# Attention weights turned through three rotating PSUM banks, with the mixed output in a bank of its own

## What is computed

```python
o_cmp, p_cmp = nsa_compressed(q, k_c, v_c, cmp_pos, cmp_w1, cmp_w2, slopes)
o_sel = nsa_selected(q, k_s, v_s, p_cmp, slopes)
o_win = nsa_window(q, k_w, v_w, slopes)
g = jax.nn.sigmoid(gate_logit.reshape(B, T, N_HEADS, 3))
o = g[..., 0:1] * o_cmp + g[..., 1:2] * o_sel + g[..., 2:3] * o_win
return o.reshape(B, T, MIX_WIDTH) * jax.nn.silu(z)
```

## Time and profile before

| what | value |
|---|---|
| median of 3 runs | 2367.28 us (2366.47 to 2367.64) |
| span of the profiled execution, first to last instruction | 2361.6 us |
| median minus that span | 5.7 us |
| busy share of the span: TensorE matmul, VectorE, ScalarE | 95%, 42%, 21% |
| the attention stage in the span, first scores to last gated output | 2173.1 to 2238.9 us |

### The profile page before, as it was taken

The page is one execution under the profiler, slowest core; times in us unless marked ns, Lnnn a source line. Parts: engine busy times, 40 slices in busy tenths (PEclk is TensorE's granted clock), DMA queues, the critical chain, the costliest instruction groups (busy, mean ns, idle before and its releaser), DMA issues.

```text
span 2361.6 us, 31308 instructions
## 1 busy us (share of the span) xinstructions
PE 2247.6 (95%) x13240; PEld 1193.1 (51%) x13240; DVE 998.6 (42%) x1839; ACT 504.0 (21%) x909; POOL 6.0 (0%) x10
## 2 busy tenths in 40 slices
PE   8999999999999989998999999899999999999797
PEld 2443454444443335756444433337884447786545
DVE  6569543211112117975011112136752446545574
ACT  3275000211111102142111111111112321113601
POOL 0000000000000000000000000000000000000000
PEclk9999999999999999999999999999999999999999
DMA  8623435799999995284999999952221220121252
GB/s 315 224 72 123 167 133 242 291 424 427 428 427 427 426 413 214 87 344 171 401 428 427 428 427 428 427 240 72 89 90 53 81 75 27 53 80 73 69 190 72
DMA packets 73528, 565.96 MB, mean 240 GB/s; under 512 B 11081, under 2 KB 12105, under 8 KB 40683
## 3 DMA queue, kind: packets, MB, share of 16 engines
q1 hardware_dynamic: 64928, 540.33, 57.3%
q10 hardware_dynamic: 7596, 20.47, 2.3%
q0 software_dynamic: 864, 3.15, 0.3%
HBM read 547.67 MB, written 14.68 MB: 238 GB/s over the span
## 4 chain that ended last, share of the span: by engine, by line
PE 71%; DVE 12%; DMA 11%; ACT 3%; issue 2%; SPq 0%; ACTq 0%; DVEq 0%
PE bank L219 70%; DMA experts<-in_exp_w 6%; DMA fast_w<-in_w_in 2%; DMA wring<-in_w_small 1%; PE bank L222 1%; DMA cf_wmod<-in_w_mod 1%; DVE cf_y L2124 1%; DVE scores L3579 0%; DVE residual L1842 0%; ACT wring L1770 0%; DVE fast_s L2381 0%; DVE fast_s L2378 0%; DVE fast_s L2380 0%; DVE fast_s L2379 0%; ACT scores L3631 0%
## 5 line engine op out<-in xcount | busy, mean ns | idle before, releaser
L219 PE MATMUL bank<-normed,wring 128*128 128x512 f32 (+2 forms) x960 | 379.6, 579 | 0.7 <-ACT normed L377 0.5
L219 PE MATMUL bank<-experts,wring 128*64 128x512 f32 x1632 | 360.1, 594 | 15.0 <-DMA experts<-in_exp_w 14.7
L1805 DVE TENSOR_TENSOR squares<-squares,bank 128x512 f32<-128x512 f32 x32 | 22.0, 688 | 662.8 <-ACT squares L1799 662.8
L219 PEld LDWEIGHTS bank<-normed,wring 128*128 128x128 f32 (+1 forms) x960 | 158.4, 181 | 182.8 <-issue 172.9
L219 PEld LDWEIGHTS bank<-experts,wring 128*64 128x64 f32 x1632 | 115.1, 137 | 252.1 <-issue 227.8
L219 PE MATMUL bank<-experts,hs_t 128*64 128x512 f32 (+1 forms) x832 | 169.8, 562 | 0.6 <-DMA experts<-in_exp_w 0.2
L219 PE MATMUL bank<-rms,y 128*128 128x512 f32 x256 | 123.0, 604 | 4.5 <-DVE residual L1842 4.5
L1842 DVE SCALAR_TENSOR_TENSOR residual<-bank,mods,residual 128x512 f32<-128x512 f32 x128 | 96.1, 751 | 73.0 <-PE bank L219 65.7
L1799 ACT ACTIVATE squares<-bank 128x512 f32<-128x512 f32 x32 | 19.1, 597 | 483.5 <-PE bank L219 483.5
L219 PEld LDWEIGHTS bank<-experts,hs_t 128*64 128x64 f32 x832 | 58.2, 137 | 105.8 <-issue 98.6
L219 PE MATMUL bank<-proj 64*64 64x64 f32 (+1 forms) x2192 | 92.0, 233 | 5.8 <-ACT proj L3200 4.8
(11 more groups left out here) (638 smaller groups left out, 2835.6 us busy)
## 6 DMA issues: line engine op xcount, KB each, us to landing
experts<-in_exp_w SPq DMA_DIRECT2D x146, 2048.0 KB, 21.1
spare<-in_exp_w SPq DMA_DIRECT2D x20, 2048.0 KB, 21.8
normed<-in_exp_w SPq DMA_DIRECT2D x20, 2048.0 KB, 20.4
wring<-in_w_in SPq DMA_DIRECT2D x44, 512.0 KB, 4.1
wmod<-in_w_mod SPq DMA_DIRECT2D x16, 1024.0 KB, 6.2
residual<-in_w_mod SPq DMA_DIRECT2D x16, 1024.0 KB, 6.6
cf_wmod<-in_w_mod SPq DMA_DIRECT2D x16, 1024.0 KB, 9.8
fast_w<-in_w_in SPq DMA_DIRECT2D x30, 512.0 KB, 4.4
```

The source lines that it names most:

```text
L219: return self.nc.tensor.matmul(out, lhsT, rhs, start=start, stop=stop, skip_group_check=True)
L1805: k.vec(v.tensor_tensor(m.hs[:, e, :], m.hs[:, e, :], k.bank[3 - 2 * e][:, :], ALU.mult), f"{m.name}.hs{i}.{e}")
```

## The change

The blocks of each head are cut into parts of up to four blocks (`parts_of`): one part for each head in units 0 and 1, two in the others. Parts are numbered through all units (`part_number`); part x is transposed into bank 4 + x % 3, and waits for the copy of part x - 3. ScalarE waits for each part by itself and copies it with one instruction; a short block in a part with others is copied with them, on all 128 partitions. Bank 7 holds the mixed output alone, and the wait for the output of the unit before, ahead of the fifth block of head 1, is gone. Instructions after the changed functions stand 13 to 17 lines further down (the exponentials at L3648, the copies at L3658).

```diff
--- before.py
+++ after.py
@@ -3510,30 +3510,47 @@
     ins.then_inc(*k.up("tensor", f"at{n}.scores"))
 
 
+def parts_of(m, n):
+
+    last = len(blocks_of(m, UNITS[n][0])[2]) - 1
+    return [(e, o, min(o + 4, last + 1), o == last) for e in range(2) for o in range(0, last + 1, 4)]
+
+
+def part_number(m, n, i):
+
+    return sum(len(parts_of(m, x)) for x in range(n)) + i
+
+
 def turned_weights_tensor(k, m, n):
 
-    t, bank = k.nc.tensor, k.bank
-    c, hp, u = UNITS[n]
+    t, (c, hp, u) = k.nc.tensor, UNITS[n]
+    blocks = blocks_of(m, c)[2]
     t.wait_ge(*k.at(f"at{n}.weights"))
-    for e in range(2):
-        for j, (o, w, _) in enumerate(blocks_of(m, c)[2]):
-            if n and e == 1 and j == 4:
-                t.wait_ge(*k.at(f"at{n - 1}.out"))
-            ins = k.turn(bank[4 + 2 * e + j // 4][0:w, (j % 4) * P:(j % 4 + 1) * P], m.sc[:, u + e, o:o + w])
-        ins.then_inc(*k.up("tensor", f"at{n}.turned{e}"))
+    for i, (e, lo, hi, _) in enumerate(parts_of(m, n)):
+        x = part_number(m, n, i)
+        if x >= 3:
+            t.wait_ge(*k.at(f"at.part{x - 3}"))
+        for j in range(lo, hi):
+            o, w, _ = blocks[j]
+            ins = k.turn(k.bank[4 + x % 3][0:w, (j - lo) * P:(j - lo + 1) * P], m.sc[:, u + e, o:o + w])
+        ins.then_inc(*k.up("tensor", f"at.turned{x}"))
+
+
+def mixed_bank(k):
+    return k.bank[7][:, 0:P]
 
 
 def mixed_tensor(k, m, n):
 
-    t, bank = k.nc.tensor, k.bank
+    t = k.nc.tensor
     c, hp, u = UNITS[n]
     blocks = blocks_of(m, c)[2]
-    t.wait_ge(*k.at(f"at{n}.pt1"))
+    t.wait_ge(*k.at(f"at.part{part_number(m, n + 1, 0) - 1}"))
     if n:
         t.wait_ge(*k.at(f"at{n - 1}.out"))
     for j, (o, w, val) in enumerate(blocks):
         for e, r in enumerate(HALVES):
-            ins = k.mm(bank[7][r, 0:P], val, m.pt[0:w, e, j * P:(j + 1) * P], j == 0, j == len(blocks) - 1)
+            ins = k.mm(mixed_bank(k)[r, :], val, m.pt[0:w, e, j * P:(j + 1) * P], j == 0, j == len(blocks) - 1)
     ins.then_inc(*k.up("tensor", f"at{n}.mixed"))
 
 
@@ -3603,7 +3620,7 @@
     c, hp, u = UNITS[n]
     cols = slice(c * P, (c + 1) * P)
     v.wait_ge(*k.at(f"at{n}.mixed"))
-    k.vec(v.tensor_tensor(m.ys[:, 6 + hp, cols], k.bank[7][:, 0:P], m.pj[:, NZ + hp, cols], ALU.mult), f"at{n}.out")
+    k.vec(v.tensor_tensor(m.ys[:, 6 + hp, cols], mixed_bank(k), m.pj[:, NZ + hp, cols], ALU.mult), f"at{n}.out")
 
 
 def attention_vector(k, m, filler):
@@ -3634,15 +3651,11 @@
 
 def turned_weights_scalar(k, m, n):
     s = k.nc.scalar
-    c, hp, u = UNITS[n]
-    j = len(blocks_of(m, c)[2]) - 1
-    for e in range(2):
-        bb, pt = (k.bank[4 + 2 * e], k.bank[5 + 2 * e]), m.pt[:, e, :]
-        s.wait_ge(*k.at(f"at{n}.turned{e}"))
-        for o in range(0, j, 4):
-            w = min(4, j - o)
-            k.act(s.copy(pt[:, o * P:(o + w) * P], bb[o // 4][:, 0:w * P]))
-        k.act(s.copy(pt[0:NCMP, j * P:(j + 1) * P], bb[j // 4][0:NCMP, (j % 4) * P:(j % 4 + 1) * P]), f"at{n}.pt{e}")
+    for i, (e, lo, hi, alone) in enumerate(parts_of(m, n)):
+        x = part_number(m, n, i)
+        rows = NCMP if alone else P
+        s.wait_ge(*k.at(f"at.turned{x}"))
+        k.act(s.copy(m.pt[0:rows, e, lo * P:hi * P], k.bank[4 + x % 3][0:rows, 0:(hi - lo) * P]), f"at.part{x}")
 
 
 def attention_scalar(k, m, filler):
```

## The result

| what | before | with the change |
|---|---|---|
| median of five runs each, side by side | 2367.28 us (2365.81 to 2368.47) | 2374.65 us (2371.57 to 2378.08) |
| ratio, with its 95% interval | | 1.0040 (1.0029 to 1.0051) |
| the profiled execution: span | 2361.6 us | 2376.8 us (2378.08 us in all) |
| VectorE's first biases to the last gated output | 64.48 us | 73.14 us |

The account below looks back on a forecast made before the run. A circle of waits between VectorE and ScalarE was taken to set the pace. Terms -0.36 + 1.52 + 1.80 - 0.49 = +2.47 us, with one clock fall at 1.0, made +3.5: 2370.8 us, range 2367.0 to 2375.5.

Parts of the forecast that it names:

- the clock's term: TensorE's longer pauses before the fourth parts, units 2 to 6: one fall of the granted clock, +1.0 us.
- Rival 1: The clock falls in several units: three falls, +5.5 to +9.7 us, taken as 2374; chance 0.32.
- the forecast: Attention stage: the new wait binds and the clock falls at most once, +1.7 to +4.7 us; chance 0.61.
- The waits: Attention stage, sum without the clock: delays in units 2 to 6 less gains in units 0 and 7, +2.47 us.
- Unit 7: From mixed(6) to mixed(7): TensorE's own work sets 5.58 us instead of 6.07, so -0.49 us.
- Copies merged in unit 0: ScalarE's copies ahead of the gate activation: two take 1.02 us where four took 1.38, -0.36 us.
- Around the span: Outside the profiled span: 5.7 us added to get from the forecast span to the median.
- The upper bound: Transposes and scores behind a pause: one clock fall can at most double them, +2.4 us.

Follow-up runs that it names:

- e5_filled_less: The changed kernel with two unread constant matmuls ahead of the fourth part of units 2 to 6: 2368.94 us beside 2366.50, ratio 1.0009.
- e6_change_again: The changed kernel, unaltered, run again on the same chip as the filled ones: 2372.39 us beside 2366.50, ratio 1.0029.
- e4_wait_alone: The kernel before, plus a wait of head 1's fifth block for its own unit's first copy: 2375.41 us beside 2367.21, ratio 1.0032.
- e7_filled_but_one: e5_filled_less without the filling matmuls in unit 6: 2369.82 us beside 2366.50, ratio 1.0016.
- e3_filled: The changed kernel with four unread constant matmuls ahead of the fourth part of units 2 to 6: 2376.37 us beside 2367.21, ratio 1.0036.
- e1_old_banks: The changed kernel's parts and merged copies, but with the banks and wait of the kernel before: 2365.32 us beside 2367.21, ratio 0.9987.

## Why the prediction was wrong

The direction and the mechanism came out, the size didn't. **The step that failed is the clock's term**: "I take one fall, at 1.0, a little under the middle". The profile shows four falls of some 1.6 us each, 6.5 in all. Rival 1, the clock falling in several units, was the outcome; it had 0.32, the forecast 0.61. That its taken value, 2374, lies so near the measured 2374.65 is partly luck: it counted three falls, and the same kernel measured again had 2372.39.

- **The waits, forecast +2.47.** With the clock held (e5_filled_less) the units take, against before, 0.41, 0.14, 0.62 and 0.48 us more in units 2 to 5 (forecast 0.38, 0.11, 0.58, 0.45), 1.80 in unit 6 (forecast 1.80) and 0.33 less in unit 7 (forecast 0.49 less). With the 0.36 of unit 0 the sum is +2.76. Timed it is 2.4 us, or 2.1 by the ratio with -0.2 to 4.3. These terms were right.
- **Unit 7** came out 0.16 dearer: mixed(7) starts 2251.07 - 2245.33 = 5.74 us after mixed(6), and I had reckoned 5.58. TensorE's own work is what it waits for, as forecast, without a gap:

```profile
2247.38 2.04 PE L222 MATMUL bank<-consts,scores 128*128 128x128 f32 x16
2249.26 1.88 PE L219 MATMUL bank<-mixer_out,proj 128*128 128x512 f32 x4
```

  From start to start the transposes took 1.88 us, for 1.80 reckoned, and the four steps of the branch product 1.81, for 1.74.
- **Copies merged in unit 0, forecast -0.36.** The two copies take what I took them for, and the gate activation now starts at 2191.14, 1.02 us after the first copy, where before it was 1.38:

```profile
2190.12 0.99 ACT L3658 COPY scores_t<-bank 128x384 f32<-128x384 f32 x2 [0.40 <-ACT squares L2580]
```

- **The clock, forecast one fall at 1.0.** Four falls, each against the same unit of e5_filled_less: 1.62, 1.50, 1.68 and 1.70 us, 6.5 in all, and 0.14 ahead of unit 2. With the waits, 2.76 + 6.50 + 0.14 makes 9.40; 0.75 goes off, since the profiled execution of before lost that much itself ahead of unit 2 (14.26 us there, against 13.15 without a fall, plus the 0.36 that ScalarE's copies took longer); the 8.65 left stand beside 73.14 - 64.48 = 8.66. For e6_change_again it is 2.76 + 4.08 - 0.75 = 6.09 beside 6.10. This splits the difference over its causes; it is no check of them, for the terms are themselves differences between rows of the table. The check is e5_filled_less: with the clock held the falls' share is gone and the waits are the forecast's.

- **Around the span** I took 5.7 us, the median less the profiled span. In the change it is 1.3 us, so most of the 5.7 was that one execution being quicker than the median. The sum was made against the median too and isn't touched by it.

Two errors made the clock's term small. The count: from one row on either side I held a pause short of the 3.9 us of unit 0 to be half safe, and took one fall for three like pauses. It isn't that the pauses came out longer: they were 2.97 us in unit 2 (3.37 in e6_change_again) for 3.4, and 2.44 (1.46) in unit 4 for 3.1; a pause of 1.78 us in unit 3 still lost the clock. The price: I took 1.0 as the middle between nothing and 2.4, but for scores with no slack left behind them a fall costs nearly its own lost work: eight steps of the branch products took 5.29 instead of 3.60. The upper bound held: the dearest fall, in unit 5 of e6_change_again, cost 2.06.

The length of the pause alone doesn't tell which unit loses the clock. In the change 2.97, 1.78, 2.48 and 2.37 us lost it and 2.44 didn't; in e6_change_again 3.37, 2.80 and 2.48 lost it, 1.46 and 1.58 didn't; in e4_wait_alone 3.43, 2.12, 2.67 and 2.46 lost it, 2.08 didn't; in e7_filled_but_one the one left, 2.37, lost it. The shorter ones are oftener safe, but 1.78 wasn't, and the 3.53 us of unit 0 were safe in e6_change_again. What decides in the single case stays open. So 12 of these 16 pauses lost the clock; of the 14 that were filled, in e3_filled, e5_filled_less and units 2 to 5 of e7_filled_but_one, none did.

The Trainium skill ("TensorE: Matmul & The Clock Gate", A second HAM failure mode: psum-queue depth-cycling) tells of a kernel that cycles through banks and idles between groups often enough for the clock to swing between its two levels. The traces agree here: in units 2 to 6 the clock goes from 1.00 to 0.50 and back four times in one execution and three in another. The rotation by itself isn't what does it: e4_wait_alone rotates no bank and loses as much, 1.0032 against 1.0029 and 1.0040.

The Trainium skill ("Perfetto Trace Analysis", Optimizing Tensor Performance, Matmuls) has independent groups rotate through banks so that the copy of one overlaps the next. Here the copy has to wait for the exponentials ahead of it on ScalarE, so with three banks for four parts TensorE waited for ScalarE's list, and no copy began earlier for it (the first of unit 4 starts 1.65 us behind the output of unit 3, before 1.64); e1_old_banks, with four banks and bank 7 shared, is the quicker one: 0.9987 against 1.0040.

## What to carry to other kernels

Before a buffer's wait is moved to another engine, read what stands ahead of the releasing instruction in that engine's list, and what stands behind the waiting one: here a copy behind six exponentials held the scores that VectorE needed, and putting the scores first gave the loss back. Where a change joins several short pauses of TensorE into one in each of several like units, reckon with the clock falling in most of them (12 of 16 here), and price a fall at the lost half of the work behind the pause that has no slack. Matmuls on constants in such a pause tell how much of a loss is the clock, if they fit it: two of them, 1.98 us, did so here, four, 3.70 us, overran it and told nothing.

## What the runs showed that I had not expected

- The same code lost the clock in units 2, 3, 5 and 6 in one execution and in 2, 3 and 5 in another, with 10.31 and 8.62 us for unit 6. One fall changes the next pause: in the second execution the late fall in unit 5 left a pause of 1.58 us in unit 6, where the first had 2.37.
- A matmul of 128x512 in 32-bit floats shows as two steps: two matmuls of the filling are x4 in the timeline and take 1.98 us, four are x8 and 3.70 us.
